# Half-row norms, a merged final norm, and a new order of attention passes and recurrence steps in a one-core transformer kernel

## What is computed

```
for l in range(2):
    x = x + 0.5 * swiglu(rmsnorm(x, norm_w[l, 0]), ...)      # ffn(l,0)
    h = rmsnorm(x, norm_w[l, 1])
    x = x + (even_mixer(h, ...) if l == 0 else odd_mixer(h, ...))
    x = x + 0.5 * swiglu(rmsnorm(x, norm_w[l, 2]), ...)      # ffn(l,1)
return rmsnorm(x, final_norm_w)
```

```
proj = h @ w_in                    # 14 parts
y_a = (silu(rg) * rms_norm(retention(rq, rk, rv))) @ ret_w_out
y_b = (silu(hg) * rms_norm(hgrn2_scan(hq, log_f, h_k, hi)) * g) @ hgrn_w_out   # 8 heads, blocks of 16 tokens
y_c = swa_with_sinks(sq, sk, sv, sinks) @ swa_w_out                            # sliding window, 16 query heads
merged = sigmoid(ga) * y_a + sigmoid(gb) * y_b + sigmoid(gc) * y_c
h = layer_norm(alpha * h + merged @ w_o, ...)
ff = swiglu_2(h) if layer == 0 else moe_swiglu(h)              # 8 experts, top 2
h = layer_norm(alpha * h + ff, ...)
```

## Time and profile before

| | us |
|---|---|
| median of 3 runs (lowest, highest) | 3330.45 (3327.91, 3337.19) |
| profiled execution | 3328.18 |
| its span | 3326.1 |
| PE busy | 3113.4 (94 %) |
| DVE busy | 2401.6 (72 %) |
| ACT busy | 1790.5 (54 %) |
| POOL busy | 189.5 (6 %) |
| mean granted clock of PE | 0.962 |

### The profile page before, as it was taken

One profiled execution on the slowest core, in us unless ns is written; L12 is line 12 of the kernel. 1 busy time (PEld: TensorE's weight loads), 2 busy tenths in 40 slices (PEclk: granted clock), 3 DMA queues, 4 the chain that ended last, 5 costly groups with the idle time before them and its releaser, 6 DMA issues. The chain is left out here.

```text
span 3326.1 us, 46005 instructions
## 1 busy us (share of the span) xinstructions
PE 3113.4 (94%) x18426; PEld 2724.8 (82%) x18426; DVE 2401.6 (72%) x2700; ACT 1790.5 (54%) x2121; POOL 189.5 (6%) x101
## 2 busy tenths in 40 slices
PE   8997899998899899989998999998999999999997
PEld 6886788876688798988888998887888888888886
DVE  5655566898766666655766656556999899999997
ACT  4444444433344355544444455444777777777775
POOL 0000000002300001110000021100000000000000
PEclk9998899999999899999999999997999999999998
DMA  5542255443155433343554333435999999999995
GB/s 191 189 178 92 102 190 199 176 161 119 70 187 190 174 140 116 139 143 132 179 189 158 141 137 128 143 127 198 360 355 354 354 356 353 354 357 352 356 358 201
DMA packets 97703, 698.65 MB, mean 210 GB/s; under 512 B 10992, under 2 KB 11504, under 8 KB 14064
## 3 DMA queue, kind: packets, MB, share of 16 engines
q1 hardware_dynamic: 97520, 696.11, 56.6%
HBM read 693.97 MB, written 1.05 MB: 209 GB/s over the span
## 5 line engine op out<-in xcount | busy, mean ns | idle before, releaser
L823 PE MATMUL ps<-weight_high,act_parts 128*128 128x512 f32 (+2 forms) x2656 | 750.0, 364 | 13.7 <-DVE act_parts L2631 3.8
L823 PEld LDWEIGHTS ps<-weight_high,act_parts 128*128 128x128 f32 x2656 | 480.8, 191 | 93.0 <-issue 10.2
L823 PE MATMUL ps<-weight_low,act_parts 128*128 128x512 f32 (+2 forms) x1456 | 516.4, 355 | 0.0
L794 PE MATMUL ps<-act_parts,weight_high 128*128 128x512 f32 x1760 | 459.9, 396 | 9.1 <-DVE weight_low L649 8.4
L794 PEld LDWEIGHTS ps<-act_parts,weight_high 128*128 128x128 f32 x1760 | 319.3, 190 | 70.2 <-DVE weight_low L649 10.9
L823 PE MATMUL ps<-act_parts,weight_low 128*128 128x256 f32 x1312 | 375.1, 286 | 0.0
L602 ACT ACTIVATE weight_high<-ring 128x2048 fp32r<-128x2048 f32 x108 | 206.6, 1914 | 311.4 <-PE ps L794 232.9
L823 PE MATMUL ps<-act_parts,weight_high 128*128 128x256 f32 x1792 | 335.7, 289 | 6.9 <-DVE weight_low L2487 5.7
L649 DVE TENSOR_TENSOR weight_low<-ring,weight_high 128x2048 fp32r<-128x2048 f32 x108 | 247.3, 2290 | 126.8 <-ACT weight_high L602 126.8
L2487 DVE TENSOR_TENSOR weight_low<-ring,weight_high 128x2048 fp32r<-128x2048 f32 x82 | 190.2, 2320 | 201.1 <-PE ps L823 130.8
L823 PEld LDWEIGHTS ps<-weight_low,act_parts 128*128 128x128 f32 x1456 | 280.2, 192 | 35.7 <-issue 1.0
(11 more groups left out here) (444 smaller groups left out, 5817.0 us busy)
## 6 DMA issues: line engine op xcount, KB each, us to landing
ring<-in_l_moe_up SPq DMA_DIRECT2D x110, 1024.0 KB, 4.9
ring_more<-in_l_moe_down SPq DMA_DIRECT2D x110, 1024.0 KB, 5.0
ring<-in_l_w_in SPq DMA_DIRECT2D x92, 1024.0 KB, 4.8
vtm<-in_l_moe_gate SPq DMA_DIRECT2D x55, 1024.0 KB, 5.0
merged<-in_l_moe_gate SPq DMA_DIRECT2D x55, 1024.0 KB, 4.9
ring<-in_l_ffn_down SPq DMA_DIRECT2D x52, 1024.0 KB, 4.8
ring<-in_l_ffn_up SPq DMA_DIRECT2D x35, 1024.0 KB, 4.8
ring_more<-in_l_ffn_gate SPq DMA_DIRECT2D x32, 1024.0 KB, 4.8
```

Of the source, the lines that this page charges most:

```text
L794: return c.nc.tensor.matmul(c.ps[:, bank, :], still, c.act[:, k, :, :].rearrange("p s t -> p (s t)"), start=k == 0, stop=k == KD - 1, skip ...
L823: ins = nc.tensor.matmul(out, still[a], moving[b], start=first and n == 0, stop=last and n == 2, skip_group_check=True)
```

## The change

**Half rows.** `Rms`, `LayerNorm` and `route_stage` scale 512 columns of row block 0, 512 of row block 1, and then the other halves; `normed` counts four. The transposes follow by halves, four tiles at a time, in the order 0, 2, 1, 3; banks 4 and 5 hold tiles 0 to 3, banks 6 and 7 the others. In `Rms`, ACT's unload k waits for DVE's low part k − 2 (before: k − 4). `LayerNorm` takes both reciprocals ahead of the scaling.

**Final norm.** `final_norm_stage` goes. The first mixer's norm is a `FinalLayerNorm`: statistics of z = x·w instead of x, with both norms in one factor, since the layer norm of rmsnorm(x)·w is (z − mean z) / sqrt(var z + eps·(mean x² + rms_eps)). w comes with the tables of the FFN before, into `vtm`.

**Even stage.** ACT: the gMLP's root goes ahead of the last unload; `take_probs(s − 2)` ahead of `exps(s)`; gMLP split at s = 4; the high parts of units 11 and 12 at s = 2 and 8. DVE: `bias(s)` ahead of `factor(s − 1)`; `gm_norm` behind `factor(0)`; low parts of 11 and 12 at s = 3 and 9; gate and split at s = 4; the addition of EA to x at s = 8. PE: `out(EA)` in two tiles at s = 5 and 6, the first tile of `out(EA + 1)` at s = 9, its second behind the passes. POOL waits for the norm's four halves before its first work.

**Mixer.** `hg_scans` from PREPARE + 1 to RECUR − 3, `hg_exps` from RECUR − 3 and `hg_queries` from RECUR − 1 to RECUR − 2; `sw_take_probs(s − 2)` ahead of `sw_exps(s)`.

**Last expert step.** The first half of the down unit is split ahead of the hidden values.

```diff
@@ Rms
-        for t in range(TT):
-            nc.vector.tensor_scalar(c.work[:, D * t:D * t + D], c.x[:, t, :], c.small[:, 6 + t:7 + t], None,
-                                    ALU.mult).then_inc(self.normed.sem, 1)
+        for h in range(2):
+            for t in range(TT):
+                at = slice(512 * h, 512 * h + 512)
+                nc.vector.tensor_scalar(c.work[:, D * t:D * t + D][:, at], c.x[:, t, at], c.small[:, 6 + t:7 + t], None,
+                                        ALU.mult).then_inc(self.normed.sem, 1)
...
-            act.wait_ge(self.packed.sem, self.packed.base + k % 4 + 1)
-            if k >= 4:
-                act.wait_ge(self.low.sem, self.low.base + k - 3)
+            act.wait_ge(self.packed.sem, self.packed.base + norm_packed(k))
+            if k >= 2:
+                act.wait_ge(self.low.sem, self.low.base + k - 1)
@@ new: FinalLayerNorm(LayerNorm), statistics on DVE
+        for t in range(TT):
+            z = self.normed_rows(t)
+            link(nc.vector.tensor_tensor(z, c.x[:, t, :], self.weight, ALU.mult))
+            for h in range(2):
+                link(nc.vector.bn_stats(small[:, 32 + 16 * t + 6 * h:38 + 16 * t + 6 * h], z[:, 512 * h:512 * h + 512]))
+            link(nc.vector.bn_aggr(small[:, 16 + 2 * t:18 + 2 * t], small[:, 32 + 16 * t:44 + 16 * t]))
+        dve.wait_ge(self.rooted.sem, self.rooted.base + 1)
+        link(nc.vector.tensor_scalar(small[:, 8:10], small[:, 4:6], LN_EPS / D, LN_EPS * RMS_EPS, ALU.mult, ALU.add))
+        for t in range(TT):
+            nc.vector.tensor_tensor(small[:, t:t + 1], small[:, 17 + 2 * t:18 + 2 * t], small[:, 8 + t:9 + t], ALU.add)\
+                .then_inc(self.summed.sem, 1)
...
+        for t in range(TT):
+            last = nc.scalar.activation(c.work[:, D * (2 + t):D * (3 + t)], c.x[:, t, :], ACT.Square,
+                                        accum_out=c.small[:, 4 + t:5 + t])
@@ norm_turn becomes norm_turns
+    for h in range(2):
+        for t in range(TT):
+            pe.wait_ge(norm.normed.sem, norm.normed.base + 2 * h + t + 1)
+            for k in (4 * h, 4 * h + 2, 4 * h + 1, 4 * h + 3):
+                last = c.nc.tensor.transpose(norm_bank(c, k)[:, P * t:P * t + P], rows(t)[:, P * k:P * k + P], c.ident)
+                if t == TT - 1 and k % 4 >= 2:
+                    last.then_inc(norm.packed.sem, 1)
@@ even_stage, tensor
-                if s == OUT:
-                    out(EA, 0)
-            out(EA + 1, 0)
+                for t in range(TT):
+                    if s == OUT + t:
+                        out(EA, 0, (t,))
+                if s == OUT + 4:
+                    out(EA + 1, 0, (0,))
+            out(EA + 1, 0, (1,))
@@ even_stage, scalar
             for s in range(PASSED + 2):
+                if s == MIX + 1:
+                    for i in range(2):
+                        gm_split(i)
+                if s >= 2:
+                    take_probs(s - 2)
                 if s < PASSED:
                     exps(s)
-                if s >= 2:
-                    take_probs(s - 2)
-                if s == MIX + 2:
-                    for i in range(2):
-                        gm_split(i)
-                if s == OUT + 2:
+                if s == MIX - 1:
+                    make_high(EA + 1)
+                if s == OUT + 3:
                     make_high(EB)
@@ even_stage, vector
             bias(0)
-            gm_norm()
-            make_low(11)
             for s in range(1, PASSED + 1):
-                factor(s - 1)
-                if s < PASSED:
-                    bias(s)
                 if s == MIX + 1:
                     for b in range(2):
                         gm_gate(b)
-                if s == MIX + 2:
+                if s < PASSED:
+                    bias(s)
+                factor(s - 1)
+                if s == 1:
+                    gm_norm()
+                if s == MIX:
+                    make_low(EA + 1)
+                if s == MIX + 1:
                     for i in range(2):
                         gm_split(i)
-                if s == OUT + 2:
+                if s == OUT + 3:
                     add_x(EA, 0)
+                if s == OUT + 4:
                     make_low(EB)
@@ even_stage, gpsimd
+            pool.wait_ge(norm.normed.sem, norm.normed.base + 4)
@@ mixer_stage, scalar
-                    if u == RECUR[half] - 3:
+                    if u == RECUR[half] - 2:
                         hg_exps(half)
-                    if u == RECUR[half] - 2:
                         hg_more_exps(half)
...
+                if 0 <= s - 2 < PASSES:
+                    sw_take_probs(s - 2)
                 if 0 <= s < PASSES:
                     sw_exps(s)
-                if 0 <= s - 2 < PASSES:
-                    sw_take_probs(s - 2)
@@ mixer_stage, vector
-                    if u == PREPARE[half] + 1:
+                    if u == RECUR[half] - 3:
                         hg_scans(half)
-                    if u == RECUR[half] - 3:
                         hg_differences(half)
-                    if u == RECUR[half] - 1:
+                    if u == RECUR[half] - 2:
                         hg_queries(half)
@@ experts_stage, vector, last step
+                    units.make_low(dve, units.down(n, 0))
                     make_hidden_low(n)
-                    for j in range(2):
-                        units.make_low(dve, units.down(n, j))
+                    units.make_low(dve, units.down(n, 1))
@@ run_stage, tables of the FFN before the second block
-                  [(t[:, 0:4392], d["l_second_tables"])]][i]
+                  [(t[:, 0:4392], d["l_second_tables"]), (c.vtm[:, 0, :], d["final_norm_w"].partition_broadcast(P))]][i]
```

More of the change, by code:

```diff
@@ L315, in tensor @@
         c, nc = self.c, self.c.nc
[L316 to L318 removed]
+        norm_turns(c, self, pe, lambda t: c.work[:, D * t:D * t + D])
     def advance(self):
@@ L344, in sync, with normed_rows, statistics @@
             sp.dma_start(self.c.rowbuf[:, n, :], row.partition_broadcast(P)).then_inc(self.loaded.sem, 16)
-    def vector(self, dve):
+    roots = 0
+    def normed_rows(self, t):
+        return self.c.x[:, t, :]
+    def statistics(self, dve):
         c, nc, small = self.c, self.c.nc, self.c.small
@@ L422, in advance, with __init__, normed_rows, statistics @@
         self.scaled.advance(4)
-def norm_bank(c, k):
-    return c.ps[:, 4 + k % 4, T * (k // 4):T * (k // 4) + T]
-def norm_turn(c, norm, t, rows):
-    for b in range(4):
-        for k in (b, b + 4):
-            last = c.nc.tensor.transpose(norm_bank(c, k)[:, P * t:P * t + P], rows[:, P * k:P * k + P], c.ident)
-        if t == TT - 1:
-            last.then_inc(norm.packed.sem, 1)
+class FinalLayerNorm(LayerNorm):
+    roots = 1
+    def __init__(self, c, rows, columns, weight):
+        super().__init__(c, rows, columns)
+        self.weight = weight
+    def normed_rows(self, t):
+        return self.c.work[:, D * t:D * t + D]
+    def statistics(self, dve):
+        c, nc, small = self.c, self.c.nc, self.c.small
+        link = lambda ins: c.vchain(dve, ins)
+        for t in range(TT):
[9 more added lines that the diff above has]
+                .then_inc(self.summed.sem, 1)
+    def scalar_start(self, act):
+        c, nc = self.c, self.c.nc
+        for t in range(TT):
+            last = nc.scalar.activation(c.work[:, D * (2 + t):D * (3 + t)], c.x[:, t, :], ACT.Square,
+                                        accum_out=c.small[:, 4 + t:5 + t])
+        last.then_inc(self.rooted.sem, 1)
+        super().scalar_start(act)
@@ new lines, in norm_bank, with norm_packed, norm_turns @@
+def norm_bank(c, k):
+    return c.ps[:, 4 + 2 * (k // 4) + k % 2, T * (k % 4 // 2):T * (k % 4 // 2) + T]
+def norm_packed(k):
+    return 2 * (k // 4) + k % 2 + 1
+def norm_turns(c, norm, pe, rows):
+    for h in range(2):
+        for t in range(TT):
[4 more added lines that the diff above has]
+                    last.then_inc(norm.packed.sem, 1)
@@ L933, in project, with out @@
                 last.then_inc(made.sem, 1)
-            def out(n, bank):
+            def out(n, bank, tiles=range(TT)):
                 if n == EA:
```

140 lines of the change are left out of this document (60 added, 80 removed).

## The result

The changed kernel's median is 3273.57 us (3272.44 to 3277.21 in four runs) against 3329.18 us for the kernel before beside it: a ratio of 0.9833, 95% interval 0.9821 to 0.9845. That is 55.6 us less, where 42.4 were forecast. It lies in the forecast range of 3271 to 3307, near its lower end. The profiled execution took 3273.57 us with a span of 3271.7.

The account below looks back on a forecast made before the run. The prediction took TensorE to bound the experts and its waits on other engines to cost time elsewhere; terms of 3.2 + 4.0 + 1.2 + 14 + 8.5 + 10 + 1.5 = 42.4 us gave a median of 3288, range 3271 to 3307.

Parts of the forecast that it names:

- the walk: Even stage's twelve passes, queues followed: 17.4 us in sum, of which 14 were taken, bounds 8 and 19.
- The wait put down to the gMLP norm: Even stage: with the norm's root moved, score(2) follows at 286.2, some 6.2 us earlier.
- the bias ahead of the factor: Even stage's passes: bias(s) runs beside exps(s−1), so the last attend ends another 8.6 us earlier.
- the moved tile: Even stage's way out: unit EA+1's first tile goes between the passes, leaving 12 of 24 matmuls behind them: 2.6 us.
- the sum's first assumption: Whole kernel: the change can only be worth what PE waits for in stages other than the experts; 105 us, reachable in part.
- The term for the LayerNorms: Two LayerNorms: reciprocals +0.4 us, half row −0.35, transposes' order up to −0.9; 1.2 us gained in all, bounds 0 to 1.4.
- 3.6 forecast: Merged final norm and LayerNorm: transposes start at about 1110.1, 3.6 us earlier; the whole term was 4.0, bounds 2.5 and 4.6.
- Recurrence and sliding window: Mixers: PE's next product about 2 us earlier per half, 8.5 in all; sliding-window loop 19.8 a pair instead of 21.4, 10.
- The collisions case: Rival: moved DVE operations meet POOL's and half clock lasts through more even passes; 26 us gained, 3304, chance 0.22.
- Query products at 2 us or more: Recurrence preparation in the mixer: DVE's query products taking this long was listed as a sign that the forecast is wrong.
- ACT held at the copies: Rival, 28 passes: ACT waits at take_probs(s−2) ahead of exps(s), each pass longer by 1.1 and 1.0; 3371 us, chance 0.04.
- The case in which every stall goes: Rival, whole kernel: all upper bounds reached, 62.6 us gained, 3268, needing PE as the bound in every pass; chance 0.09.

Follow-up runs that it names:

- norms_whole: The changed kernel with whole rows scaled and the old order of transposes and banks in all norms and the router's stage: 3281.34 us, ratio 0.9859.
- pool_and_last_step: The changed kernel with POOL's wait for the even stage's norm and the last expert step's order both undone: 3279.91 us, ratio 0.9852.
- sw_undone: The changed kernel with the sliding-window passes' copy of the turned probabilities again behind the exponentials: 3283.54 us, ratio 0.9859.

## Why the prediction held, and where it was off

- **What the change reaches.** Right: the experts kept their time up to the last step, and all waits named in the earlier trace rows that were to shrink did. But the sliding window's came back in part under the names of POOL's weighing and the mask addition.
- **Even stage.** The term was 14 and the body gave 16.3, with 13.5 of idle where the walk had 17.4. Its size was nearly right and its reasons were not. The wait put down to the gMLP norm, 6.2, did go, but 4.3 of it by unit 11's parts and 2.1 by the norm's place. In idle time over the whole body the norm's place is worth 1.8 at most, the bias ahead of the factor 1.6 to 3.0, not 8.6, and the moved tile 2.8 to 4.2, not 2.6, since it covers a locked weighing. "DVE's moved make_low … where POOL and PE have a mix or a way out to do" was right of PE and wrong of POOL.
- **Clock.** The forecast lies 12.0 us short of the 54.4 that the span lost, and two errors stand behind that, of which one partly hides the other. The idle time that came back is 34.3, 8.1 less than the sum of 42.4. And the sum's first assumption failed, that a stall is worth its idle time and the clock only takes away: PE's busy time fell by 20.1. Where PE has no idle time to lose, this is plain. The first units of the two mixers took 111.4 both before and take 109.4 and 109.7; the last step gave 2.9 of its 4.5 in busy time. Both are the change's, since `norms_whole` (111.6 and 111.3) and `pool_and_last_step` bring them back. The router's 2.7 and the 1.5 behind the first sliding window aren't, as they come and go in kernels with the same code there. So part of the 55.6 is chance.
- **Norms.** The term for the LayerNorms was too low (1.2 against 4.0 with their first units, of which 0.8 is idle time). From the first transpose to the first product it is 3.41 instead of 4.26, as worked out, by the order of the transposes; the half row's 0.35 is eaten by the reciprocal ahead of it, as said.
- **Final norm.** Transposes behind 9.31 of idle instead of 13.30: 4.0 in place of 3.6 forecast.
- **Router's stage.** 0 was forecast and 2.6 measured, but it isn't shown to be the change's: from the first router matmul to the experts' first steps it took 16.1 us before and in nine of the kernels run after it, and 13.2 to 13.4 in the changed kernel and three others, among them kernels with the same code here on both sides. The granted clock there is 0.50 where it takes 16.1 and 0.63 where it takes 13.4. The experts behind it take some of it back: up to their last step they last 899.9 to 900.3 behind the short router stage and 898.7 to 899.5 behind the long one. PE's rows of the 32 router matmuls in the changed kernel and in `sw_undone`, whose router stage is the same:

```profile
2236.47 4.12 PE L2932 MATMUL ps<-tables,hT 128*128 128x8 f32 x32
```

```profile
2246.08 6.84 PE L2932 MATMUL ps<-tables,hT 128*128 128x8 f32 x32
```

- **Recurrence and sliding window.** 8.5 and 10 forecast, 8.4 and 8.7 measured, and undoing them gives 9.9 and 10.0. The mechanisms are the ones named, but the recurrence's size is in part luck: the term was a later start of PE's products, that is idle time, and of the 8.4 only 4.8 is idle. The sliding window's pace came out as worked out, 20.0 against 19.8.
- **Rivals.** The collisions case has its mechanism shown but not its price. "Query products at 2 us or more" was to be a sign of a wrong forecast, and it came true, since DVE's second still takes 3.43; the new places are worth 10 us in spite of it. ACT held at the copies did not come about. The case in which every stall goes did not come about either: 18.2 us of PE's waits now name POOL's weighing in the passes.

## What to carry to other kernels

Where TensorE waits in many short stalls, look also at what the shorter stall does to the clock of the matmuls behind it. Don't add up a walk's parts as if each had its own price: undo them one by one, and compare with several kernels that have the code in question unchanged. An elementwise product that is handed to GpSimd beside DVE products of SBUF operands can save DVE nothing if both are due together: here, on DVE alone four products took 4.6 us instead of 6.8, and the kernel 15 us less. In this kernel's LayerNorms the order in which tiles are turned moved the first product by 0.85 us, and scaling by half rows alone by nothing.

## What was not expected of the hardware

The same code differs between kernels, and executions of one kernel, by where stretches of half clock fall: an unchanged router stage takes 13.4 or 16.1 us, an unchanged even body 141.3 to 147.0, an unchanged odd mixer 124.8 to 129.4, and one kernel's four runs lie 9 us apart in two pairs (mean clocks 0.973 and 0.974 in one, 0.976 and 0.977 in the other). What sets these stretches off in one kernel and not in another with the same code is not shown. So an edit of under some 7 us is read from its stretch, with its idle time and its busy time apart, and not from the total; and even the stretch's length needs several kernels with the same code beside it.
